# A hybrid decoder trunk on one core: the first layer's b matrices scaled and spread by GpSimd in place of VectorE

## What is computed

```python
def s5_mixer(u, lam_re, lam_im, log_step, b_re, b_im, c_re, c_im, d_skip, w_glu):
    ...
    mag = jnp.exp(lr * step)
    a_re = mag * jnp.cos(li * step)
    a_im = mag * jnp.sin(li * step)
    den = lr * lr + li * li
    nr = a_re - 1.0
    f_re = (nr * lr + a_im * li) / den
    f_im = (a_im * lr - nr * li) / den
    ...
    bb_re = f_re[..., None] * br - f_im[..., None] * bi
    bb_im = f_re[..., None] * bi + f_im[..., None] * br
    x_re = jnp.einsum('bsgi,gpi->bsgp', ug, bb_re)
    x_im = jnp.einsum('bsgi,gpi->bsgp', ug, bb_im)
    ...
```

## Time and profile before

| | us |
|---|---|
| median of 3 runs | 995.14 |
| range of the runs | 994.49 to 995.17 |
| profiled execution | 994.98 |
| its span | 993.3 |
| TensorE busy in it | 950.7 |
| VectorE busy | 743.3 |
| ScalarE busy | 565.7 |
| GpSimd busy | 340.1 |

### The profile page before, as it was taken

The page is one execution under the profiler, slowest core; times in us unless marked ns, Lnnn a source line. Parts: engine busy times, 40 slices in busy tenths (PEclk is TensorE's granted clock), DMA queues, the critical chain, the costliest instruction groups (busy, mean ns, idle before and its releaser), DMA issues.

```text
span 993.3 us, 17232 instructions
## 1 busy us (share of the span) xinstructions
PE 950.7 (96%) x6447; PEld 817.6 (82%) x6447; DVE 743.3 (75%) x1240; ACT 565.7 (57%) x905; POOL 340.1 (34%) x267
## 2 busy tenths in 40 slices
PE   6899899998999999999999999999999999999997
PEld 5789666776878999999989976777777799999996
DVE  5989999985666767677865679998747676666666
ACT  6435665757454555555564466766764555555544
POOL 0111666672330573156400046667516001111010
PEclk9999999999999999999999999999999999999999
DMA  8963433335454755555469433234545445555551
GB/s 226 235 216 92 132 118 128 123 90 170 137 169 158 202 180 201 170 193 186 131 165 262 146 109 126 87 129 123 155 139 170 135 140 200 193 187 173 199 178 43
DMA packets 135864, 156.83 MB, mean 158 GB/s; under 512 B 16400, under 2 KB 103032, under 8 KB 135800
## 3 DMA queue, kind: packets, MB, share of 16 engines
q1 hardware_dynamic: 135800, 155.98, 50.3%
HBM read 154.92 MB, written 1.05 MB: 157 GB/s over the span
## 4 chain that ended last, share of the span: by engine, by line
PE 71%; DVE 16%; ACT 6%; issue 3%; POOL 2%; DMA 1%; SPq 0%; DVEq 0%; ACTq 0%; POOLq 0%; PEldq 0%
PE pj L734 51%; PE bX L734 6%; PE bA L734 5%; DVE wl L1554 5%; PE bB L734 4%; PE bY L1083 2%; DVE s5x L1883 1%; ACT wh L1260 1%; DVE work L1847 1%; PE bY L734 1%; DVE bnat L1883 1%; POOL s5h L2142 1%; PE bX L1072 1%; DVE gate L1570 1%; DVE hl L1576 1%
## 5 line engine op out<-in xcount | busy, mean ns | idle before, releaser
L1554 DVE TENSOR_TENSOR wl<-ring,wh 128x1024 fp32r<-128x1024 f32 (+1 forms) x276 | 364.6, 1324 | 134.8 <-ACT wh L1260 133.3
L1260 ACT ACTIVATE wh<-ring 128x1024 fp32r<-128x1024 f32 (+1 forms) x276 | 288.9, 1048 | 243.3 <-PE pj L734 200.6
L734 PE MATMUL pj<-hh,wh 128*128 128x256 f32 x1024 | 293.2, 286 | 6.2 <-DVE wl L1554 4.3
L734 PE MATMUL pj<-hl,wh 128*128 128x256 f32 x1024 | 289.7, 283 | 0.0
L734 PE MATMUL pj<-hh,wl 128*128 128x256 f32 x1024 | 289.6, 283 | 0.0
L734 PEld LDWEIGHTS pj<-hh,wh 128*128 128x128 f32 x1024 | 196.2, 192 | 11.2 <-issue 5.6
L734 PEld LDWEIGHTS pj<-hl,wh 128*128 128x128 f32 x1024 | 196.3, 192 | 1.2 <-issue 0.5
L734 PEld LDWEIGHTS pj<-hh,wl 128*128 128x128 f32 x1024 | 196.3, 192 | 0.0
L734 PE MATMUL pj<-wh,hl 128*128 128x512 f32 (+1 forms) x416 | 168.6, 405 | 6.6 <-DVE wl L1554 1.9
L734 PE MATMUL pj<-wh,hh 128*128 128x512 f32 (+1 forms) x416 | 159.7, 384 | 0.0
L734 PE MATMUL pj<-wl,hh 128*128 128x512 f32 (+1 forms) x416 | 159.4, 383 | 0.0
(11 more groups left out here) (315 smaller groups left out, 1471.3 us busy)
## 6 DMA issues: line engine op xcount, KB each, us to landing
ring<-in_ffn_w_up SPq DMA_DIRECT2D x44, 1024.0 KB, 5.1
ring<-in_w_in SPq DMA_DIRECT2D x40, 1024.0 KB, 5.1
ring<-in_ffn_w_down SPq DMA_DIRECT2D x22, 1024.0 KB, 5.0
ring<-in_w_in SPq DMA_DIRECT2D x16, 512.0 KB, 5.2
ring<-in_w_branch SPq DMA_DIRECT2D x8, 1024.0 KB, 5.1
ring<-in_w_out SPq DMA_DIRECT2D x8, 1024.0 KB, 5.1
ring<-in_w_branch SPq DMA_DIRECT2D x8, 512.0 KB, 6.1
ring<-in_w_in SPq DMA_DIRECT2D x8, 256.0 KB, 5.1
```

The costliest lines, as they stand in the source:

```text
L734: return nc.tensor.matmul(o, a, b, start=start, stop=stop, skip_group_check=True)
L1260: A(dst, src, ACT.Copy).then_inc(w_hi.sem, 1)
L1554: TT(dst, src, hi.bitcast(F32), ALU.subtract).then_inc(w_lo.sem, 1)
```

## The change

VectorE's `s5_b()` and its call go, and so do the clearing of bx and the semaphore bx_clear. GpSimd calls `spread_b(0)` directly behind `spread_c(0)`.

```diff
@@ -400,7 +400,6 @@
-        bx_clear = sem("bx_clear")
@@ -1674,22 +1673,6 @@
-            def s5_b():
-
-                v.wait_ge(mats_in.sem, mats_in.at(0, 16 * 6))
-                f, g = w3(tiles_of(fr, 0)), w3(tiles_of(fi, 0))
-                TT(bb[:, 0], bnat[:, 0], f, ALU.mult)
-                TT(bbt[:, 0], bnat[:, 1], g, ALU.mult)
-                TT(bb[:, 1], bnat[:, 1], f, ALU.mult)
-                stepped(TT(bbt[:, 1], bnat[:, 0], g, ALU.mult))
-                TT(bb[:, 0], bb[:, 0], bbt[:, 0], ALU.subtract)
-                stepped(TT(bb[:, 1], bb[:, 1], bbt[:, 1], ALU.add))
-                v.wait_ge(bx_clear.sem, 1)
-                for c in range(2):
-                    nc.vector.tensor_copy(bx[0:STATES, c, :, 0:GCH], bb[0:STATES, c])
-                    nc.vector.tensor_copy(bx[STATES:P, c, :, GCH:2 * GCH], bb[STATES:P, c])\
-                        .then_inc(bx_ready.sem, bx_ready.up())
-
@@ -1745,8 +1728,6 @@
                 split_lo(l, 10)
-                if l == 0:
-                    s5_b()
                 for s in range(11, 13):
@@ -2106,8 +2087,8 @@
             for l in range(DEPTH):
                 if l == 0:
-                    nc.gpsimd.memset(bx, 0.0).then_inc(bx_clear.sem, bx_clear.up())
                     spread_c(0)
+                    spread_b(0)
```

## The result

| | us |
|---|---|
| before, median of 11 runs | 995.14 (994.40 to 995.96) |
| changed, median of 11 runs | 997.88 (996.99 to 999.07) |
| ratio, 95% interval | 1.0027 (1.0018 to 1.0035) |
| changed, profiled execution | 998.38, span 996.6 |

The kernel became 2.7 us slower; 997.5 us was predicted, with a range of 995.2 to 999.6 us.

A forecast was written before the change was run, and what follows sets the result against it. TensorE, 96% busy, was taken as the bound, waiting for VectorE at the head. Ten pauses (4.2 us) ahead of pieces 9 and 10 turn a 1.6 us gain into a 2.4 us loss: 995.14 + 2.4 = 997.5 us, range 995.2 to 999.6 us.

The forecast's parts named there:

- What the change removes: Ten VectorE instructions, 3.49 us, between the wl of pieces 10 and 11; gain at most 1.6 us, other 1.9 us hidden.
- What the pause costs and how many there are: Ten added GpSimd instructions each pause VectorE 0.42 us before the wl of piece 10, 4.2 us in all.
- the sum: Tally in order of time: piece 9 1.7 us late, piece 10's wl 4.2 us late, first rotation 2.4 us late.
- upper bound: Two instructions on s5h alone may pause VectorE 0.54 us each: 4.5 us in all, 2.7 us at the end.
- lower bound: GpSimd instructions meeting gaps where VectorE waits for itself cost less: 3.9 us in all, 2.1 us at the end.
- Where they lie: The 4.2 us of pauses precede pieces 9 and 10; the 3.5 us removed lie behind: a loss of 2.4 us.
- Carried to the end undiminished: Behind piece 11 all engines and loads follow TensorE, so the 2.4 us reach the kernel's end whole.
- as forecast: The main case, kernel time 996.9 to 998.3 us; chance 61%.
- The whole instruction blocks: Rival: each GpSimd instruction pauses VectorE 0.62 us, 6.2 us in all, 4.4 us at the end, 999.5 us; 8%.
- No pauses: Rival: GpSimd runs in VectorE's shadow where it matters, so only the removal counts: 993.4 us; 7%.
- Part is given back: Rival: a later transfer-bound stretch absorbs up to 2 us, or fewer than seven pauses occur: 995.2 to 996.9 us; 20%.
- The clock falls: Rival: TensorE's clock halves after its stalls, each piece up to 2.9 us more; one such piece gives 1000.4 us; 4%.

The follow-up runs named there:

- e1: Changed kernel, but GpSimd only sets bx to zero and neither multiplies nor spreads the first layer's b: 993.70 us, kernel before beside it 995.52 us.
- e3: Changed kernel, but GpSimd begins spread_b(0) only when VectorE has done the wl of piece 10: 994.41 us, kernel before beside it 995.52 us.
- e7: Changed kernel, but the six products wait for the wl of piece 10 and the four spreads follow GpSimd's k rotations: 994.17 us, kernel before 995.58 us.
- e10: The changed kernel measured again, unaltered: 998.81 us, kernel before beside it 995.40 us.
- e8: Changed kernel with the four spreads as tensor_scalar, one value per partition, in both layers: 997.29 us, kernel before beside it 995.58 us.
- e5: Changed kernel, but spread_b(0) stands behind GpSimd's part of all four rotations: 999.02 us, kernel before beside it 995.58 us.
- e2: Kernel before, VectorE's s5_b kept, plus the same ten GpSimd instructions behind spread_c into tiles nobody reads: 999.28 us, kernel before 995.52 us.
- e6: Changed kernel with the six products on GpSimd, but two memsets of bx instead of the four spreads: 996.32 us, kernel before beside it 995.58 us.

## Why the prediction held, point by point

**What the change removes** (1.6 us at piece 11, 1.7 us at the rotation, the rest hidden): e1 gave 1.7 us at the rotation and 1.8 us in the median. That the DMA of piece 12 would not take it back held too.

**What the pause costs and how many there are.** Ten of 0.42 us made 4.2 us; 4.07 us were measured in the changed kernel and 4.1 us with the addition alone. The number of pauses was right, the price of single ones was not. A pause in a wl costs 0.31 us; the prediction's own rows had 1.52 us for 1.23 us, 0.29 us, and it took 0.42 us even so. That made piece 9 1.7 us late in the sum, and it was 1.45 us. The two instructions on s5h alone did cost more (0.53 us), which was the upper bound's reason, and two table instructions met a gap (0.59 and 0.72 us, a pause of 0.3 us each), the lower bound's. That these cancel to within 0.1 us is in part luck.

**Where they lie.** Pieces 9 and 10 late, piece 11 without a wait, +2.4 us at the rotation: measured +2.4 us. e3 and e7 show that the place is the cause: the same instructions behind the wl of piece 10 leave it where it was.

**Carried to the end undiminished.** In the medians it is +2.7 us, on another chip +3.4 us (e10), which is outside "as forecast" though inside the range. The profiled execution ended 3.4 us later than the one before; 1.8 us of this was there at the rotation (0.6 us of head start included), and the rest came in two steps, 0.9 us behind 114 us and 0.6 us behind 598 us, where the clock fell. So the loss of 2.4 us that was forecast is shown at the rotation; how near the median comes to it depends also on the clock, which the sum put at nothing.

**The whole instruction blocks** (pauses of 0.62 us, 6.2 us in all): refuted by the measured 15.01 - 10.94 = 4.07 us. **No pauses**: refuted by the same 4.07 us. **Part is given back**: nothing of it was.

**The clock falls** was the rival that I weighed wrong, at 4%, on the ground that the clock was full through the first wait of 5.3 us and in every slice; the slices are too coarse for it. It did fall behind waits of 1.9 to 3.1 us: at a cost in e10, e8 and e5, for free in e2 and in the changed kernel's first profile. In e6 it did not fall, behind waits of 1.44 and 2.14 us. The price that I gave, up to 2.9 us for a piece, was too high: a piece lost 1.5 us, and two pieces together lost 1.5 us in e10.

## What to carry to other kernels

Work moved from VectorE to GpSimd was not free for VectorE: each two-input GpSimd instruction on 128x256 elements that met VectorE's two-input instructions put a pause of 0.3 to 0.5 us into VectorE here, 0.41 us on average. So ask of such a move not only when GpSimd is idle, but what VectorE has to deliver in that time: put it behind the last result that another engine waits for, and count the pauses. The same change was a loss of 2.4 us at the first rotation with its ten pauses ahead of that, and a gain of 1.4 us in the median with them behind it.

## What was not expected of the hardware

- The granted clock fell to 1.2 GHz after TensorE had waited only 2.1 us (rows of the changed kernel and e10), not in every run (not in e6 behind 2.14 us) and not at the same piece. What it costs depends on what stands behind it: nothing when the next piece has to wait anyway, 1.5 us when it hasn't.
- A GpSimd multiplication by one value per partition took 1.19 us on 128x256 elements, the one of two tensors 0.62 us beside an idle VectorE, and yet it cost VectorE about a third as much.
- Where both engines had two-input instructions queued, they took turns one for one, so the count of GpSimd's instructions set VectorE's delay. GpSimd waits as well: one of its instructions beside a wl takes 1.6 us, beside a short table instruction 0.67 us. In e8, with the one-input form on GpSimd, they did not: four of its instructions stood beside eight of VectorE's.
